# Small products in TensorE's opening pauses, and a weight difference moved behind the turned context's lower halves

## The chip, the cores and the metric

One core of a Trainium2 chip runs the whole program. The metric is the device time in microseconds of one execution, the median of three. TensorE (PE) does the matrix products, ScalarE (ACT) and VectorE (DVE) the element work, GpSimd (POOL) small things, and SyncE (SP) issues nearly all weight loads.

## The reference, cut to what matters

The model is a first block with an adaptive norm, followed by two more layers. Every product is of 256 tokens with a float32 weight. Only the opening matters here: the conditions' modulation and the first gated layer of the context.

```python
def ada_in(x, mod, j, g):
    return rmsnorm(x, g) * (1 + mod[:, 3 * j + 1, None]) + mod[:, 3 * j, None]
...
    sc = jax.nn.silu(c)
    scc = jax.nn.silu(c_ctx)[None]
    mod = (sc @ w_mod[l] + b_mod[l]).reshape(-1, N_MOD, D_MODEL)
    modc = (scc @ w_mod[l] + b_mod[l]).reshape(1, N_MOD, D_MODEL)
...
    xc = ada_out(xc, swiglu(ada_in(xc, modc, 0, norm_pre[l, 0]), ffn_w_in[l, 0], ffn_w_out[l, 0]),
                 modc, 0, norm_post[l, 0], 0.5)
```

`w_mod` has 1024 rows and 9 x 1024 columns, `ffn_w_in` 1024 rows and 2 x 2816 columns.

## The kernel before, in words

**Precision.** A float32 product is made of three faster ones. A factor is split into an upper half (rounded, `whi` for weights, `cTh` for the context) and a lower half (the difference, `wlo`, `cTl`). ScalarE makes the upper halves, VectorE the lower ones with one subtraction each (`Vector.fill`, L2134, for weights; `lo`, L2202, for activations). TensorE then does upper x upper, lower x upper and upper x lower.

**Loads.** SyncE brings weights into a ring of four raw buffers of 1 MB (`Sync`, L725). In this text the loads are counted from 0. Loads 0 to 3 are pieces of `w_mod`, load 4 is the first piece of `ffn_w_in`, loads 5 to 8 are `w_mod` again, and loads 9, 10, 11 are `ffn_w_in`. Load n goes where load n-4 was, so SyncE waits until that one has been read: for a `w_mod` piece by TensorE, for an `ffn_w_in` piece until VectorE has made the lower halves of both its parts. SyncE waits in order: a late load holds back all behind it. An `ffn_w_in` load is two dma instructions of 512 KB and holds two parts ("parts" 0 and 1 in load 4, 2 and 3 in load 9, 4 and 5 in load 10, 6 and 7 in load 11).

**Modulation.** `Tensor.mod` makes 512 columns of a modulation from two loads. For each it issues four products of the 32 columns of `m.sct` (the conditions, of which two columns are filled) with 512 columns of raw float32 weight, into the four groups of 32 rows of one bank. VectorE adds the bias (`modr`, L2278), and `Tensor.settle` brings the rows into columns (the `selm` products, 128x2). VectorE copies them to `modc` (the shift, L2339) or makes `gcol` of them (the gain, L2342).

**The opening's order.** `Tensor.first_block` runs modulation 0 (loads 0, 1) and 1 (loads 2, 3), turns the normed context with sixteen transposes (L992) into four banks (`sh0`), does modulation 2 (loads 5, 6), then part 0, modulation 3 (load 7, the settling of 2, load 8), part 1, the settling of 3, and parts 2 to 7 back to back (`OPENING`). A part is 24 products of 128x256 and waits (`split`) for its own lower half. Parts 0 to 3 read the context's first four column blocks ("half 0"), parts 4 to 7 the last four ("half 1"). No product is done without data of its own being there, so TensorE stands still between the first loads.

`Vector.first_block` (L2498 and on) runs twice over a half. In each round it adds the biases, makes the weight differences of two parts (`force(2 + 2 * half)`), settles the gain, multiplies and shifts a turned half (L2247) while ScalarE does the other token tile (L1602), and takes the context's lower halves (`cTl`) of both tiles after ScalarE's `cTh`.

Of the kernel before, what the change touches and what calls it, by code (L numbers as in the profile page):

```python
# [90 lines left out]
class Tables:  # L91
# [96 lines left out]
    def mod(self, nb, bank=None):  # L188
        self.take("mod", nb, bank=bank)
        self.mod_units[nb] = len(self.units)  # L190
        for kh in range(2):
            self.mod_read[len(self.units)] = (nb, kh, len(self.mod_units))
            self.unit([(slice(0, 2048), 4, self.I["w_mod"][kh * 512:kh * 512 + 512, nb * 512:nb * 512 + 512].rearrange("(k p) n -> p k n", p=128))], 0, 0)
        self.settle()
        self.open = nb
# [686 lines left out]
class Tensor:  # L882
# [139 lines left out]
        elif s in (0, 2):  # L1022
            self.e.wait_ge(self.m.xt_done, self.ready[i] - (s == 0))

    def mod(self):
        m, e = self.m, self.e
        n, nb = self.nmod, MODS[self.nmod]
        u0 = self.t.mod_units[nb]
        if n == 0:
            e.wait_ge(m.c_silu, 1)  # L1030
        bank, full = self.bank("mod", nb)
        for kh in range(2):
            e.wait_ge(m.raw_in[(u0 + kh) % NRAW], self.t.raw_value[u0 + kh])
            for k in range(4):
                ins = self.mm(bank[32 * k:32 * k + 32, :], m.sct[:, 4 * kh + k, :], m.raw[:, (u0 + kh) % NRAW, k * 512:k * 512 + 512],
                              kh == 0, kh == 1)
            ins.then_inc(full if kh else m.mod_half, 1)
            if kh == 0:
                self.settle()
        self.nmod += 1  # L1040

    def settle(self):
# [86 lines left out]
    def first_block(self):  # L1129
        m, e = self.m, self.e  # L1130
        cT, xT = (m.cTh, m.cTl), (m.xTh, m.xTl)
        self.mod()
        self.mod()
        e.wait_ge(m.ld_ident, 16)
        for half in range(2):
            for i in range(2):
                e.wait_ge(m.normed, 2 * i + half + 1)
                self.turned(("sh0", 2 + i), half, m.zc[:, i, :])
                self.settle()
        self.nn, self.nx = 4, 4  # L1140
        self.mod()
        for n, (g, kh) in enumerate(OPENING):
            e.wait_ge(m.xt_done, 4 if kh else 2)
            for v in range(2):
                self.sub_w(2 * n + v, ("up", "c", g), 2 * kh + v, cT, 256, 4, 2, 512)
                if n == 0:
                    if v == 0:
                        self.mod()
                    else:
                        self.settle()  # L1150

        def ahead_c(g):
            if 4 <= g < EARLY:
                self.mod()
        self.hidden("c", cT, 2, ahead_c, lambda g: None, between={
            4: lambda: self.shape_z(("sh0", 0), 0), 7: lambda: self.shape_z(("sh0", 1), 1), 12: lambda: self.summed(10)})
        self.own(2, 0)
        self.own(2, 1)
        self.hidden("x", xT, 0, lambda g: None, self.beside, 6, {(1, 2 * NG - 6 + 4): lambda: self.shape_z(("sh1", 0), 0)},
                    {12: lambda: self.summed(12)})  # L1160
        self.latent()
        self.renewed(2)
        order = [(("wo1", half), 2 * kh + v, 2 * (1 - kh) + v) for kh in (1, 0) for half in range(2) for v in range(2)]
        self.product([("wo1", 0), ("wo1", 1)], xT, 2, 4, 2, 512, self.mixed, tail=6, order=order, hooks={
            (0, 3): lambda: self.heads("ml", m.Mh, 1), (0, 5): self.settle, (1, 6): lambda: self.shape_z(("sh", 1, 0), 0)})
        self.ffn(1, xT, lambda i: self.shape_z(("sh", 1, i), i), lambda: self.shape_x(("sh", 2, 0), 0), 6, 6, (5, 4))
# [936 lines left out]
class Vector:  # L2103
# [376 lines left out]
    def first_block(self):  # L2480
        m, e = self.m, self.e
        e.memset(m.brow[:, :, :], 0.0).then_inc(m.dve, 1)
        e.memset(m.sct[:, :, :], 0.0).then_inc(m.dve, 1)
        e.memset(m.cols[:, NCOL:NCOL + 2], -0.5).then_inc(m.dve, 1)
        for _ in range(3):
            self.step()
        e.wait_ge(m.ld_cols, 16)
        self.normalize()
        self.mod()
        self.normalize()  # L2490
        for half in range(2):
            if half:
                self.mod()
            self.mod()
            self.force(2 + 2 * half)
            self.settle()
            self.evacuated("mod2", half, 0)
            self.evacuated("mod2", 2 + half, 0)  # L2498
            self.shift(("sh0", 3), half, 0, 1)
            for i in range(2):  # L2500
                self.shifted(m.cTl, m.cTh, i, (half,))
        self.stream(8, between={5: lambda: self.hide("c", 0)})
        self.hide("c", 1)
        for g in range(2, NG):
            if 4 <= g < EARLY:
                self.mod()
            self.stream(4)
            self.settle()
            self.hide("c", g)
            if g in (6, 7):  # L2510
                self.normalize()
        e.memset(m.selm[:, 130:258], 1.0).then_inc(m.dve, 1)
        self.step()
        self.hidden(NG - 1)
        st, floor = [self.stat() for _ in range(2)], [0, 0]

        def weigh(half, i):
            c = slice(half * 512, half * 512 + 512)
            self.squared()
            bank, free = self.held("dn", "c", 0, half, i)  # L2520
            e.tensor_tensor(m.z[:, i, c], bank[:, :], m.gp[:, 1, c], ALU.mult).then_inc(free, 1)
            if half == 0:
                e.tensor_scalar(st[i][:, 0:1], st[i][:, 0:1], D * EPS, None, ALU.add).then_inc(m.dve, 1)
                floor[i] = self.step()

        for u in range(2 * NG):
            self.force(self.used + 1)
            if u == NG - 1:
                for i in range(2):
                    weigh(0, i)  # L2530
            self.use()
            if u in (4, 7):
                self.shape(("sh0", u // 5), 0, 0, (m.xTh, m.xTl))
            if u == 15:
                self.summed(10)

        def post(i):
            weigh(1, i)
            for half in range(2):
                self.evacuated("dn", "c", 0, half, i)  # L2540
            self.post(m.xc[:, i, :], m.z[:, i, :], st[i], 0.5, floor[i])

        beside = {0: {0: lambda: post(0), 2: self.normalize}, 1: {0: lambda: post(1), 2: self.normalize},
                  5: {0: lambda: self.biased("c", m.Rc), 1: lambda: self.conv1(m.uPc, m.uc), 2: lambda: self.logged("c", m.Rc, 1)},
                  6: {0: lambda: self.run("c", m.Rc, 0, m.po_dve), 2: self.context_out},
                  7: {1: lambda: self.context_values(0)}, 8: {1: lambda: self.context_states(0), 2: lambda: self.context_values(1)},
                  9: {1: lambda: self.context_states(1)}}
        for g in range(NG):
            self.stream(4, between=beside.get(g, {}))
            if g == 0:  # L2550
                self.summed(11)
            self.hide("x", g)
            self.beside(g)
        self.hidden(NG - 1)
        gp = [[m.gp[:, n, :]] * 2 for n in range(2)]
        self.last(NG, [[("dn", "x", 0, half, i) for i in range(2)] for half in range(2)], gp[0], True,
                  lambda: self.shape(("sh1", 0), 1, 0, (m.xTh, m.xTl)), 6, "x", between={15: lambda: self.summed(12)})
        self.latent()
        self.last(4, [[("wo1", half, i) for i in range(2)] for half in range(2)], gp[1], True,
                  lambda: self.shape(("sh", 1, 0), 2, 0, (m.xTh, m.xTl)), 6, "wo1", late=True)  # L2560
        self.ffn(1, False, gp[0], False, lambda: self.gained(("sh", 2, 0), 0), 6, 6, 5, "ffn1")
# [503 lines left out]
```

## Time and profile before

| | us |
|---|---|
| median of three runs (lowest, highest) | 2028.65 (2028.09, 2030.54) |
| the profiled execution's own time | 2027.45 |
| its span, first to last instruction | 2025.6 |
| TensorE busy in it | 1993.3 (98%) |

Times of the trace count from the first instruction. The span lacks 1.85 us of what the execution is timed at. The first 50 us hold all that the change touches.

### The profile page before, as it was taken

Reading aid. Unit: us, or ns where it says so; the run is one execution under the profiler, and the core shown is the slowest. Engines: PE = TensorE matmul, PEld = TensorE weight load, DVE = VectorE, ACT = ScalarE, POOL = GpSimd, SP = SyncE. Lnnn points to the kernel's source line nnn. Section 1 sums busy time; section 2 is a strip of 40 time slices with the busy share of each in tenths; the row PEclk is TensorE's granted clock in tenths of the full one; section 3 lists DMA queues with packets and bytes.
Section 4 is the critical chain, followed back from the end, with each engine's and each line's share of the span. In section 5 each row is a group of like instructions: output and inputs, shape, how many; then the busy total and the mean of one; then the engine's idle time right before and its main releaser. Section 6 shows DMA issues by size and latency. Waiting matters only on the chain.

```text
span 2025.6 us, 27588 instructions
## 1 busy us (share of the span) xinstructions
PE 1993.3 (98%) x10892; PEld 1687.4 (83%) x10892; DVE 1351.2 (67%) x2199; ACT 1104.2 (55%) x1722; POOL 60.3 (3%) x125
## 2 busy tenths in 40 slices
PE   7999999999999999999999999999999999999998
PEld 5988899988678888888997888888888897788887
DVE  4457676666787656655598896655665587987653
ACT  4344465445565446554646766545654646666552
POOL 0000000001000000000100000000000100000000
PEclk9999999999999999999999999999999999999999
DMA  9797755675268656655543466555755534457551
GB/s 338 257 299 255 238 188 178 213 256 174 96 203 259 208 176 216 196 177 198 199 143 125 141 217 218 187 178 161 233 177 202 203 117 150 142 189 237 187 179 51
DMA packets 281905, 392.90 MB, mean 194 GB/s; under 512 B 9612, under 2 KB 175932, under 8 KB 281648
## 3 DMA queue, kind: packets, MB, share of 16 engines
q1 hardware_dynamic: 277616, 379.62, 57.0%
q0 software_dynamic: 3184, 9.02, 1.4%
q10 hardware_dynamic: 976, 2.49, 0.3%
q8 instruction: 87, 1.43, 0.3%
q14 instruction: 42, 0.34, 0.0%
HBM read 390.04 MB, written 1.05 MB: 193 GB/s over the span
## 4 chain that ended last, share of the span: by engine, by line
PE 83%; DVE 6%; issue 4%; DMA 3%; ACT 3%; POOL 0%; SPq 0%; DVEq 0%; POOLq 0%; ACTq 0%
PE bank L944 20%; PE bank L946 20%; PE bank L945 20%; PE bank L908 19%; DMA raw<-in_ffn_w_in 2%; DVE wlo L2134 1%; PE bank L1084 1%; DVE junk L2837 1%; PE bank L992 1%; ACT whi L1531 1%; DMA raw<-in_w_mod 1%; DVE wlo L2139 1%; ACT whi L1536 0%; DVE tm L2994 0%; ACT junk L1591 0%
## 5 line engine op out<-in xcount | busy, mean ns | idle before, releaser
L2134 DVE TENSOR_TENSOR wlo<-raw,whi 128x1024 fp32r<-128x1024 f32 x360 | 435.4, 1223 | 279.1 <-ACT whi L1531 273.3
L1531 ACT ACTIVATE whi<-raw 128x1024 fp32r<-128x1024 f32 x360 | 376.5, 1058 | 381.7 <-PE bank L946 223.4
L944 PE MATMUL bank<-whi,xTh 128*128 128x512 f32 (+1 forms) x1344 | 528.7, 393 | 3.9 <-DVE xTl L2202 2.0
L946 PE MATMUL bank<-whi,xTl 128*128 128x512 f32 (+1 forms) x1344 | 520.6, 387 | 0.0
L945 PE MATMUL bank<-wlo,xTh 128*128 128x512 f32 (+1 forms) x1344 | 520.1, 387 | 0.0
L2139 DVE SCALAR_TENSOR_TENSOR wlo<-raw,cols,whi 128x512 fp32r<-128x512 f32 (+2 forms) x608 | 407.1, 722 | 149.7 <-ACT whi L1536 146.4
L1536 ACT ACTIVATE whi<-raw,cols 128x512 fp32r<-128x512 f32 (+2 forms) x608 | 385.6, 696 | 147.0 <-PE bank L946 110.4
L944 PEld LDWEIGHTS bank<-whi,xTh 128*128 128x128 f32 x1344 | 252.6, 188 | 57.4 <-issue 4.4
L946 PEld LDWEIGHTS bank<-whi,xTl 128*128 128x128 f32 x1344 | 252.4, 188 | 52.4
L945 PEld LDWEIGHTS bank<-wlo,xTh 128*128 128x128 f32 x1344 | 252.8, 188 | 48.9 <-issue 0.5
L908 PE MATMUL bank<-xTh,whi 128*128 128x256 f32 x696 | 197.9, 284 | 0.0
L908 PE MATMUL bank<-xTl,whi 128*128 128x256 f32 x696 | 196.9, 283 | 0.0
L908 PE MATMUL bank<-xTh,wlo 128*128 128x256 f32 x696 | 196.9, 283 | 0.0
L944 PE MATMUL bank<-whi,hThb 128*128 128x512 f32 x352 | 138.0, 392 | 0.0
L946 PE MATMUL bank<-whi,hTlb 128*128 128x512 f32 x352 | 137.1, 389 | 0.0
L945 PE MATMUL bank<-wlo,hThb 128*128 128x512 f32 x352 | 137.0, 389 | 0.0
L908 PEld LDWEIGHTS bank<-xTh,whi 128*128 128x128 f32 x696 | 133.5, 192 | 1.2 <-issue 1.0
L908 PEld LDWEIGHTS bank<-xTl,whi 128*128 128x128 f32 x696 | 133.5, 192 | 0.4 <-issue 0.2
L908 PEld LDWEIGHTS bank<-xTh,wlo 128*128 128x128 f32 x696 | 133.5, 192 | 0.0
L908 PE MATMUL bank<-cTh,whi 128*128 128x256 f32 x392 | 112.5, 287 | 1.2 <-DVE wlo L2134 1.1
L908 PE MATMUL bank<-cTl,whi 128*128 128x256 f32 x392 | 110.9, 283 | 0.0
L908 PE MATMUL bank<-cTh,wlo 128*128 128x256 f32 x392 | 110.8, 283 | 0.0
(372 smaller groups left out, 2432.8 us busy)
## 6 DMA issues: line engine op xcount, KB each, us to landing
raw<-in_w_in SPq DMA_DIRECT2D x68, 1024.0 KB, 5.2
raw<-in_ffn_w_in SPq DMA_DIRECT2D x132, 512.0 KB, 5.7
raw<-in_ffn_w_gate SPq DMA_DIRECT2D x88, 512.0 KB, 4.1
raw<-in_ffn_w_up SPq DMA_DIRECT2D x88, 512.0 KB, 5.1
raw<-in_ffn_w_down SPq DMA_DIRECT2D x40, 1024.0 KB, 5.0
raw<-in_w_mod SPq DMA_DIRECT2D x36, 1024.0 KB, 5.3
raw<-in_ffn_w_out SPq DMA_DIRECT2D x30, 1024.0 KB, 5.7
raw<-in_w_out SPq DMA_DIRECT2D x12, 1024.0 KB, 5.1
```

Of the source, the lines that this page charges most:

```text
L908: return self.e.matmul(o, lhsT, rhs, start=start, stop=stop, skip_group_check=True)
L944: e.matmul(o, hi[:, kc, sl], wh[:, c], start=at == 0 and k == 0, stop=False)
L945: e.matmul(o, hi[:, kc, sl], wl[:, c], start=False, stop=False)
L946: ins = e.matmul(o, lo[:, kc, sl], wh[:, c], start=False, stop=fin)
L992: ins = self.e.transpose(bank[:, c * 128:c * 128 + 128], src[:, k * 128:k * 128 + 128], self.m.ident[:, :])
L1084: ins = e.transpose(bank[:, (2 * c + i) * 128:(2 * c + i + 1) * 128], htok[:, 2 * (g % 2) + i, c * 128:c * 128 + 128], m.ident[:, :])
L1531: e.activation(wh, raw, ACT.Copy).then_inc(m.whi_done, 1)
L1536: ins = e.activation(wh[:, c], raw[:, c], ACT.Copy, scale=m.cols[:, a + k:a + k + 1])
L2134: e.tensor_tensor(wl, raw, wh.bitcast(F32), ALU.subtract).then_inc(m.wlo_done, 1)
L2139: ins = e.scalar_tensor_tensor(out=wl[:, c], in0=raw[:, c], scalar=m.cols[:, a + k:a + k + 1], in1=wh[:, c].bitcast(F32), op0=ALU.mult, op ...
L2837: ins = e.scalar_tensor_tensor(out=y[:, c, :], in0=m.uC[:, c, j:j + 256], scalar=w_, in1=y[:, c, :], op0=ALU.mult, op1=ALU.add)
```

## The change

`Tensor.warm` issues a number of products of 32 by 256 columns of `m.sct` with itself, into the four row groups of the bank in which the last turned half will be put later; nothing reads their results. There are 28 of them behind modulation 0's first half, 8 behind its second, and 8 behind modulation 1's first half (and the settling of modulation 0 that follows that).

In `Vector.first_block` each round now makes only the first of its two weight differences ahead of the shift; the second stands behind the context's lower halves. In round 0 that is the difference of part 1, in round 1 that of part 3. ScalarE's order and TensorE's order of everything else stay.

```diff
+    def warm(self, count):
+
+        m = self.m
+        bank = m.psum[self.t.bank["sh0", 3, 1][0]]
+        for k in range(count):
+            self.mm(bank[32 * (k % 4):32 * (k % 4) + 32, 0:256], m.sct[:, k % 8, :], m.sct[:, :, :].rearrange("p k s -> p (k s)"), True, True)
+
-    def mod(self):
+    def mod(self, fill=(0, 0)):
...
             if kh == 0:
                 self.settle()
+            self.warm(fill[kh])
...
-        self.mod()
-        self.mod()
+        self.mod((28, 8))
+        self.mod((8, 0))
         e.wait_ge(m.ld_ident, 16)
...
             if half:
                 self.mod()
             self.mod()
-            self.force(2 + 2 * half)
+            self.force(1 + 2 * half)
             self.settle()
             self.evacuated("mod2", half, 0)
             self.evacuated("mod2", 2 + half, 0)
             self.shift(("sh0", 3), half, 0, 1)
             for i in range(2):
                 self.shifted(m.cTl, m.cTh, i, (half,))
+            self.force(2 + 2 * half)
```

## Rows read from the trace of the kernel before

**Rows 1.** The page: busy time of each engine over the span.

```profile
PE 1993.3 (98%) x10892; PEld 1687.4 (83%) x10892; DVE 1351.2 (67%) x2199; ACT 1104.2 (55%) x1722; POOL 60.3 (3%) x125
```

**Rows 2.** Chain of waits, 0 to 120 us: start, length, engine and line.

```profile
26.34 12.09 PE bank L908 x96
...
44.74 23.28 PE bank L908 x192
```

**Rows 3.** Timeline of TensorE: start, length, instruction, count, idle time before it.

```profile
6.96 1.93 PE L908 MATMUL bank<-raw,sct 128*32 128x512 f32 x8 [6.96 <-DMA raw<-in_w_mod]
12.73 1.94 PE L908 MATMUL bank<-raw,sct 128*32 128x512 f32 x8 [3.84 <-DMA raw<-in_w_mod]
15.33 1.94 PE L908 MATMUL bank<-raw,sct 128*32 128x512 f32 x8 [0.67 <-DMA raw<-in_w_mod]
17.20 1.87 PE L908 MATMUL bank<-selm,modr 128*128 128x2 f32 x8
...
23.54 2.80 PE L992 MATMUL bank<-ident,zc 128*128 128x128 f32 x12
...
28.48 0.39 PE L908 MATMUL bank<-cTh,whi 128*128 128x256 f32 x1
...
31.54 1.06 PE L908 MATMUL bank<-raw,sct 128*32 128x512 f32 x8
...
32.54 1.05 PE L908 MATMUL bank<-selm,modr 128*128 128x2 f32 x8
...
38.43 0.36 PE L908 MATMUL bank<-cTh,whi 128*128 128x256 f32 x1
```

**Rows 4.** Windows of the trace: busy time of each engine, granted clock, DMA share, GB/s.

```profile
13.00:15.00 2.00, 1.67 (x8) 0.00 (x0) 1.42 (x8) 1.75 (x6) 0.00 (x0) 1.00 1.05 387
...
28.00:30.00 2.00, 2.00 (x20) 1.52 (x13) 1.03 (x2) 0.00 (x0) 0.29 (x1) 1.00 1.05 385
...
46.00:48.00 2.00, 2.00 (x19) 2.00 (x18) 2.00 (x2) 0.24 (x2) 0.00 (x0) 1.00 0.58 177
```

**Rows 5.** Timeline of SyncE's issues: loads 6, 7, 8, and one issued at 53 us.

```profile
17.33 0.37 SPq L725 DMA_DIRECT2D raw<-in_w_mod  x1
...
20.99 0.37 SPq L725 DMA_DIRECT2D raw<-in_w_mod  x1
...
24.65 0.37 SPq L725 DMA_DIRECT2D raw<-in_w_mod  x1
...
53.10 0.37 SPq L725 DMA_DIRECT2D raw<-in_w_mod  x1
```

**Rows 6.** The same four issues in the DMA view: size, us to landing.

```profile
raw<-in_w_mod SPq DMA_DIRECT2D x1, 1024.0 KB, 9.5
...
raw<-in_w_mod SPq DMA_DIRECT2D x1, 1024.0 KB, 8.4
...
raw<-in_w_mod SPq DMA_DIRECT2D x1, 1024.0 KB, 7.5
...
raw<-in_w_mod SPq DMA_DIRECT2D x1, 1024.0 KB, 5.2
```

**Rows 7.** Timeline of VectorE and ScalarE, 21 to 46 us.

```profile
22.26 2.36 DVE L2134 TENSOR_TENSOR wlo<-raw,whi 128x1024 fp32r<-128x1024 f32 x2 [0.36 <-ACT whi L1531]
...
27.05 1.29 DVE L2202 TENSOR_TENSOR cTl<-full,cTh 128x512 fp32r<-128x512 f32 x2 [0.82 <-ACT cTh L1585]
...
36.02 2.01 ACT L1531 ACTIVATE whi<-raw 128x1024 fp32r<-128x1024 f32 x2 [8.48 <-DMA raw<-in_ffn_w_in]
...
37.11 2.36 DVE L2134 TENSOR_TENSOR wlo<-raw,whi 128x1024 fp32r<-128x1024 f32 x2 [1.52 <-ACT whi L1531]
...
41.89 1.29 DVE L2202 TENSOR_TENSOR cTl<-full,cTh 128x512 fp32r<-128x512 f32 x2 [0.83 <-ACT cTh L1585]
...
43.37 4.63 DVE L2134 TENSOR_TENSOR wlo<-raw,whi 128x1024 fp32r<-128x1024 f32 x4 [0.18 <-ACT whi L1531]
```

**Rows 8.** Waits of SyncE, 0 to 30 us: total, times, longest.

```profile
SPq L725 <- DVE wlo L2134: 3.3, 1, 3.3
```

## The prediction

> **What bounds the kernel now.** The page comes first: TensorE is busy for 98% of the span [rows 1], so a microsecond won or lost in its queue is won or lost at the end, unless a transfer or another engine takes it back on the way. The chain of waits says where this holds in the opening: from 26.34 to 38.43 us and from 44.74 to 68.02 it runs in TensorE alone [rows 2]. Nothing that moves the start of parts 4 to 7 (44.74) is hidden behind them, and the four raw buffers tie the later loads to TensorE's own progress. So the question is when part 4 starts.
>
> The timeline shows two things ahead of that. TensorE waits for `w_mod` three times: 6.96, 3.84 and 0.67 us [rows 3]. And the same eight records of a modulation half take 1.93 us at first and 1.06 us at 31.54, the settling 1.87 and 1.05 us [rows 3]. Early TensorE works at half its later rate, that of the lower of its two clock levels, although the windows print a granted clock of 1.00 throughout [rows 4]; I go by the durations. Under all this lies a third bound: the DMA engines are fully used, 387 GB/s at 13 us and 385 at 28, and let up only at 46 us (share 0.58) [rows 4]. A load then lands when those ahead of it have landed, whenever TensorE becomes ready.
>
> **Step 1, the small products.** A modulation half is four products of 512 columns in 1.93 us; four of 256 columns should take half, about 0.97 at the low rate and 0.53 at the high one. 28 are seven such groups: 3.7 us if all are fast, 6.8 if all are slow. The pause is 3.84 us. Work at the low rate ran from 12.73 to 26.3 without the rate rising, but it held a gap of 0.67 us and settlings that stream two columns [rows 3]. The small products make an unbroken stretch of real streaming from 6.96 us on, so I take it that the rate doubles somewhere in them, that they end near 13 to 14.5 us, and that TensorE is fast from there. Cost at this point: up to 2 us on load 1's products, and load 5 is issued later by as much; load 4 and those ahead keep the DMA busy meanwhile, so this is hidden. The two groups of eight cost 2 x 0.53 us each and lie in waits for loads 2 and 3. Bounds: nothing, or (all slow) the rival below.
>
> What does the faster rate bring? Modulation 2's second load, 6, is issued at 17.33 and lands 9.5 us later, at 26.83 [rows 5, 6]. Its products then take 1.06 us, to 27.9, where part 0 starts today at 28.48 [rows 3]. The gain is at most 0.6 us, because the DMA sets the rest. This is the term in which the whole first edit ends.
>
> **Step 2, round 0 of VectorE.** The two differences start at 22.26 and take 2.36 us [rows 7]. With one of them moved, the shift and the context's lower halves come 1.2 us earlier: they end at 27.05 + 1.29 = 28.34 now, and at about 27.15 then. That is before 27.9, so it allows the 0.6 us of step 1 and no more. Part 1's difference then ends at about 28.35; TensorE wants part 1 only after part 0 and modulation 3, beyond 34 us, so for TensorE it is hidden.
>
> It isn't for SyncE. Load 8 goes where load 4 was and waits for both differences: that is SyncE's wait of 3.3 us on `wlo` [rows 8], ended at 24.65 [rows 5]. Now it ends at 28.4. Load 7, the one ahead, lands at 20.99 + 8.4 = 29.4 [rows 5, 6], so the queue holds one microsecond of work, a fresh load shows 5.2 us from issue to landing [rows 6], and load 8 lands at 28.4 + 5.2 = 33.6 instead of 24.65 + 7.5 = 32.15: 1.45 us late. Loads 9, 10 and 11 are issued behind it. The bound below is no gap at all (28.4 is still before 29.4), that above 1.45 us for load 9 too. I take 1.0, nearer to the fresh load's row. The Trainium skill, "DMA: Bandwidth & Descriptors", section on the anatomy of one DMA, fits a fixed 2.0 us and then bytes at 436 GB/s; by its 4.4 us for this load, load 8 would be only 0.7 us late and my total below 0.3 to 0.5 us smaller. The trace's 5.2 us is of a HBM-to-SBUF load of exactly this size and disagrees, so I keep it.
>
> On TensorE: part 0 27.9 to 30.8 (2.9 us, as (38.43 to 44.3) / 2), load 7's products and the settling 1.06 + 1.05 to 32.9, then 0.7 us of waiting for load 8, its products to 34.7, part 1 to 37.6, the settling to 38.6. Part 2 started at 38.43. The 0.6 us are gone.
>
> **Step 3, round 1 of VectorE.** Here the moved difference is that of part 3, and part 3 follows part 2 directly. Today VectorE takes both from 37.11 to 39.47 [rows 7], part 2 runs 38.43 to 41.3, part 3 finds its difference there. Then comes the context: from the end of the differences (39.47) to the end of `cTl` (41.89 + 1.29 = 43.18) pass 3.7 us. After the change the first difference ends at 38.3, plus load 9's lateness of 1.0 is 39.3; the context's lower halves end at 43.0; part 3's difference, 1.2 us more, at 44.2; part 3 starts at 44.35 (the step from 44.59 to 44.74 today [rows 2, 7]) and not at 41.3. TensorE stands still for 2 us. Part 4 starts 2.9 later, at 47.25, against 44.74: **+2.5 us**. What the edit brings forward, the lower halves of half 1 for part 4, isn't late today by more than the third of a microsecond before 44.74, and part 4's own difference still queues behind part 3's. With no gap in the DMA the same sum gives 38.3 + 3.7 + 1.2 + 0.15 + 2.9 = 46.25, +1.5; with 1.45 us it gives +3.0.
>
> **Sum.** 0 for steps 1 and 2, +2.5 for step 3 with the late load in it: 2027.45 + 2.5 = 2029.95. The profiled execution was 1.2 us quicker than the median. I add 0.35 of that, because I expect part of the 1.2 to be a rate that rises later than in this profile, which the small products would end, and say 2030.3, 0.08% above the median.
>
> **Rivals.** *Faster: the late rise was the common case.* In the profile the rate is still low at 23.5 us, where twelve transposes take 2.80, and the next modulation half at 31.54 is fast [rows 3]. The three runs spread over 2.45 us. If in most executions the rate rises only during parts 0 and 1, the kernel before loses up to 2.9 us there (a part at half rate takes 2.9 more), and the change gives it back. With 2 us of it, and no DMA gap (+1.5), the end is 2028.65 - 2 + 1.5 = 2028.1. It decides from 1.5 us on. For it: the median above the profiled time; against: only by 1.2. Chance 0.14.
>
> *The rate falls again.* Faster products leave longer pauses, about 2 us between modulation 2's halves. If part 0 and modulation 3 then run at the low rate, that is 2.9 + 1.1 + 1.0 more, of which 0.7 lie in the wait for load 8 and the rest delays part 2 by up to 4; the rise comes back on the way, so I count half, 2 us in part 2, 1 of them under load 9's lateness: 2031.3. The Trainium skill's "TensorE: Matmul & The Clock Gate", part on the PE-mode transpose, says that transposes do not count as activity, which would favour this rival, as they lie right before. The trace here speaks against it: the stretch before the rate rose was made mostly of them. Chance 0.11.
>
> *The small products don't do what they are for.* They run slow and don't raise the rate: 6.8 us in a pause of 3.84, and 1.9 for each eight. Load 1's products start at 15.7, modulation 1 ends near 26, the transposes near 31.7, part 0 starts 5 us later than today, and part 4 some 6 later: 2034. Chance 0.07.
>
> **Chances.** My forecast has 0.68 with a range of its own of 2028.9 to 2031.8 (+1.5 to +3.0 on the profiled time, and up to 1.2 for how it stands to the median). A difference of about 0.2% (4.1 us) is what a measurement of this kernel can tell from none. Only the last rival passes it on the slow side: with tails 0.09 slower. Faster by 4.1 us isn't reached even by the first rival: 0.03. The rest, 0.88, is within. The range of 2027.7 to 2032.8 reaches into the first two rivals and leaves out the third.
>
> **What would show it.** Right: seven groups of small products whose length halves on the way; load 6's products in 1.06 us and part 0 at 27.9; SyncE's issue of load 8 near 28.4 and its landing near 33.6; a wait of TensorE of about 2 to 3 us on `wlo` near 42 us; part 4 near 47. Wrong: TensorE without a wait before part 3, load 8 landing at 32.2 as before, small products that keep 0.97 us per group, or parts 0 and 1 at half rate.

## The result: 2033.08 us, 0.24% slower

The changed kernel takes 2033.08 us in the median of seven runs (2030.23 to 2035.97), the kernel before 2028.65 in seven. The ratio is 1.0024 with a 95% interval of 1.0015 to 1.0033. The forecast was 2030.3 with a range to 2032.8: right in direction, too small in size. Measured once more beside other kernels (`after_again`) the ratio was 1.0018 (1.0009 to 1.0027).

The profiled execution took 2034.81 us, 7.36 more than that of before, span 2033.0 against 2025.6. Most of it, 6.1 us, is made in the opening. First TensorE's timeline in the changed kernel (columns as in [rows 3]).

```profile
8.57 3.94 PE L908 MATMUL bank<-sct 128*32 128x256 f32 x56
12.61 1.07 PE L908 MATMUL bank<-raw,sct 128*32 128x512 f32 x8
...
15.21 1.06 PE L908 MATMUL bank<-raw,sct 128*32 128x512 f32 x8 [0.68 <-DMA raw<-in_w_mod]
...
25.09 1.07 PE L908 MATMUL bank<-raw,sct 128*32 128x512 f32 x8 [2.66 <-DMA raw<-in_w_mod]
27.67 1.94 PE L908 MATMUL bank<-raw,sct 128*32 128x512 f32 x8 [1.52 <-DMA raw<-in_w_mod]
29.54 0.58 PE L908 MATMUL bank<-cTh,whi 128*128 128x256 f32 x1
...
34.53 1.07 PE L908 MATMUL bank<-raw,sct 128*32 128x512 f32 x8
...
46.47 0.39 PE L908 MATMUL bank<-cTh,whi 128*128 128x256 f32 x1 [2.06 <-DVE wlo L2142]
```

The small products do what they are for: the modulation half that took 1.94 us at 12.73 takes 1.07, and the groups fit their pauses. But new pauses of 2.66 and 1.52 us stand beside modulation 2, and its second half runs at 1.94 us again. The windows of the same kernel (columns as in [rows 4]) show the clock behind this.

```profile
24.00:27.00 3.00, 1.07 (x8) 0.19 (x8) 2.08 (x8) 2.43 (x7) 0.00 (x0) 1.00 1.05 384
28.00:30.00 2.00, 2.00 (x10) 0.46 (x3) 1.61 (x3) 0.00 (x0) 0.00 (x0) 0.50 0.20 72
30.00:32.00 2.00, 2.00 (x11) 2.00 (x11) 0.47 (x1) 0.00 (x0) 0.52 (x1) 0.50 0.74 160
34.00:36.00 2.00, 2.00 (x18) 1.03 (x17) 0.00 (x0) 0.00 (x0) 0.00 (x0) 1.00 1.10 369
44.00:47.00 3.00, 0.94 (x8) 0.74 (x7) 3.00 (x4) 3.00 (x4) 0.00 (x0) 1.00 0.67 211
48.00:50.00 2.00, 2.00 (x11) 2.00 (x11) 1.82 (x2) 0.00 (x0) 0.00 (x0) 0.50 0.98 304
52.00:54.00 2.00, 2.00 (x19) 2.00 (x18) 1.23 (x1) 0.19 (x1) 0.00 (x0) 1.00 0.99 324
```

The granted clock is 0.50 (1.2 GHz) in the rows from 28 to 32 us and once more at 48, behind a stretch in which TensorE stood still (0.94 of 3 us busy). While it is low, TensorE does 10 or 11 products in 2 us instead of 18 to 20. The share of the DMA is 0.20 at 28 to 30 us where it was 1.05 [rows 4]: the gap ahead of load 8. VectorE and ScalarE answer to [rows 7].

```profile
22.21 2.00 ACT L1539 ACTIVATE whi<-raw 128x1024 fp32r<-128x1024 f32 x2 [3.11 <-DMA raw<-in_ffn_w_in]
...
26.95 1.29 DVE L2210 TENSOR_TENSOR cTl<-full,cTh 128x512 fp32r<-128x512 f32 x2 [0.82 <-ACT cTh L1593]
28.16 1.22 DVE L2142 TENSOR_TENSOR wlo<-raw,whi 128x1024 fp32r<-128x1024 f32 x1
...
38.73 1.23 DVE L2142 TENSOR_TENSOR wlo<-raw,whi 128x1024 fp32r<-128x1024 f32 x1 [0.16 <-ACT whi L1539]
...
43.99 1.29 DVE L2210 TENSOR_TENSOR cTl<-full,cTh 128x512 fp32r<-128x512 f32 x2 [0.82 <-ACT cTh L1593]
45.20 4.62 DVE L2142 TENSOR_TENSOR wlo<-raw,whi 128x1024 fp32r<-128x1024 f32 x4
```

Load 4's upper halves begin at 22.21; the kernel before, in `before_again`, has them at 21.28 and every kernel without small products at 21.1 to 21.3. So load 4 lands 1 us later, which the forecast did not have. The last row is part 3's difference and those behind it: it starts where the lower halves end, and TensorE waits 2.06 us for it. SyncE's wait for load 4's differences is 9.8 us, not 3.3 [rows 8]:

```profile
SPq L725 <- DVE wlo L2142: 9.8, 1, 9.8
```

The ledger, in starts on TensorE after minus before: part 0 +1.06 (29.54 against 28.48), of which 0.9 is modulation 2's half at the low clock; modulation 3's first half, behind part 0, +2.99 (34.53 against 31.54), so part 0 costs 1.93 more; then 2.06 us of waiting for part 3, 1.7 for 3.4 us at the low clock behind it, and less 0.33, the wait ahead of part 4 that goes. That sums to 6.4; the settling of the fourth modulation group, at 92.91 us before, comes at 99.04, +6.13, so the terms overlap by 0.3 us. This ledger is of one execution, one of the slower ones; the median of the runs is only 4.4 us above that of before. A later settling, at 254.22, comes at 261.58: +7.36, the whole difference.

### The profile page after: what moved, and what is told of

The parts are those of the page before. It is cut to its first block, busy times and chain, and to the rows that moved or that the text cites. A ratio compares the mean times of both kernels' runs of the same rounds, so it can differ in the third digit from the quotient of the medians.

```text
span 2033.0 us, 27764 instructions
## 1 busy us (share of the span) xinstructions
PE 1997.1 (98%) x10980; PEld 1690.9 (83%) x10980; DVE 1351.6 (66%) x2199; ACT 1104.6 (54%) x1722; POOL 60.0 (3%) x125
## 3 DMA queue, kind: packets, MB, share of 16 engines
HBM read 390.04 MB, written 1.05 MB: 192 GB/s over the span
## 4 chain that ended last, share of the span: by engine, by line
PE 83%; DVE 6%; issue 4%; DMA 3%; ACT 3%; SPq 0%; POOL 0%; DVEq 0%; POOLq 0%; ACTq 0%
PE bank L944 20%; PE bank L946 20%; PE bank L945 20%; PE bank L908 20%; DMA raw<-in_ffn_w_in 2%; DVE wlo L2142 1%; DMA raw<-in_w_mod 1%; PE bank L1092 1%; DVE junk L2846 1%; ACT whi L1539 1%; PE bank L992 1%; DVE wlo L2147 1%; SPq L725 0%; ACT whi L1544 0%; DVE tm L3003 0%
```

## The experiments

Two settlings of TensorE's timeline serve as marks: one near 93 us, just behind the parts of the opening and before the loads of the next stage get scarce, and one near 254 us. The marks and the waits between are from one profile each, the ratios from all runs. Two executions of the kernel before differ by 0.2 us at the first mark and 1.1 at the second.

| kernel | mark at 93 | mark at 254 | ratio to before (95% interval) |
|---|---|---|---|
| before / `before_again` | 92.91 / 93.12 | 254.22 / 253.14 | 1.0005 (0.9995, 1.0015) |
| changed / `after_again` | 99.04 / 95.98 | 261.58 / 258.25 | 1.0024 (1.0015, 1.0033) / 1.0018 (1.0009, 1.0027) |
| `e1_fill` | 93.89 | 255.22 | 1.0009 (1.0000, 1.0018) |
| `e2_move` | 96.13 | 256.55 | 1.0014 (1.0005, 1.0023) |
| `e4_move1` | 96.06 | 256.36 | 1.0014 (1.0005, 1.0023) |
| `e7_hold` | 93.17 | 256.63 | 1.0017 (1.0008, 1.0026) |
| `e8_hold_move` | 96.06 | 258.18 | 1.0032 (1.0023, 1.0041) |
| `e9_hold_late5` | 93.34 | 255.84 | 1.0017 (1.0008, 1.0026) |
| `e10_mid` | 93.23 | 253.29 | 1.0003 (0.9995, 1.0012) |
| `e13_fat` | 94.04 | 256.64 | 1.0010 (1.0001, 1.0019) |
| `e15_tiny` | 93.27 | 254.91 | 1.0007 (0.9998, 1.0015) |
| `e14_fat_mid` | 92.58 | 255.32 | 1.0008 (0.9999, 1.0017) |

The first theory was that two things cost: the clock falling in the pauses that fast products leave, and part 3 standing still for its difference.

**One half each.** `e1_fill` keeps the small products and puts VectorE's order back, `e2_move` does the reverse, `e4_move1` moves only part 3's difference, without small products.

```diff
 e1_fill:             self.force(2 + 2 * half)
 e2_move, e4_move1:   self.mod((0, 0))
                      self.mod((0, 0))
 e4_move1:            self.force((1 if half == 1 else 2) + 2 * half)
                      ...
                      self.force(2 + 2 * half)
```

> Only the small products; VectorE's order as in the kernel before. Theory A (TensorE's rate falls in the pauses that faster products leave): the granted clock rises within the 28 small products, falls to 0.50 near 27 us after two pauses beside modulation 2, part 0 runs at the low rate; part 3 finds its difference and no second fall follows; part 4 near 47 to 48 us instead of 44.74, about +2 to +3 us in the end. Rival B (only the moved difference costs): part 4 at 44.7 or earlier, time within 0.5 us of before. Rival C (earlier issue of load 5 makes load 4 and 6 land later): load 4's upper halves start near 22.2 us instead of 21.2 and modulation 2's second half near 27.7 here too.

> Only the moved differences, in both rounds; no small products. Theory A: the early clock is as in the kernel before (it rises somewhere from 27 to 31 us), part 3 waits about 2 us for its difference and the clock may fall once after this wait; part 4 near 46.5 without a second fall and near 48 with one: +1.8 to +3.5 us. Rival B: the whole loss of the change is here, +4.4 us or more. Rival C: load 4's upper halves start at 21.2 as before.

> Only round 1's difference (part 3) moved; no small products. Theory A: all of the loss of e2_move is in this round, because round 0's move costs only a late load 8 that TensorE does not feel: same time as e2_move within 1 us. Rival D (load 8 held back in round 0 costs as much): this kernel is 1 us or more faster than e2_move, with load 9 landing at 36 here and at 37 there.

`e1_fill` runs modulation 2's second half low again (27.71, 1.93 us), does not wait for part 3, and is 1.0 us late at the first mark, less than the 2 to 3 us expected. Its load 4 is late too (upper halves at 22.41), which is the sign of rival C. `e2_move` waits 1.71 us for part 3 and is 3.2 late there; `e4_move1` waits as long and is 3.15 late. Two of TensorE's rows with an idle time in `e2_move`, and `e4_move1`'s wait for part 3 with the clock behind it:

```profile
34.82 1.06 PE L908 MATMUL bank<-raw,sct 128*32 128x512 f32 x8 [0.90 <-DMA raw<-in_w_mod]
...
45.04 0.39 PE L908 MATMUL bank<-cTh,whi 128*128 128x256 f32 x1 [1.71 <-DVE wlo L2142]
```

```profile
43.49 0.39 PE L908 MATMUL bank<-cTh,whi 128*128 128x256 f32 x1 [1.76 <-DVE wlo L2142]
```

```profile
44.00:47.00 3.00, 3.00 (x16) 3.00 (x16) 2.83 (x3) 0.33 (x1) 0.00 (x0) 0.51 0.73 228
```

The two sums have different terms: `e2_move` pays 0.90 us for the late load 8 and starts part 3 at 45.04, without a fall of the clock; `e4_move1` starts it at 43.49, and the clock falls behind the wait (0.51 in its row of that window). The times came as expected (2031.28 and 2031.41 us), the reasons only in part: TensorE does feel the late load 8, and part 4 starts at 48.02 us in `e2_move` though its clock did not fall. That the two times agree is partly luck, since one has a fall and the other a late load. By the marks the moved differences cost more (3.2 us) than the small products (1.0 us); the ratios, 1.0014 and 1.0009, point the same way, but their intervals overlap. Of the 3.15 us of `e4_move1`, 1.7 are its fall, by the count of the ledger above.

**The change again, and the clock held.** `after_again` is the changed kernel unchanged. `e7_hold` adds small products to `e1_fill` beside modulation 2, `e8_hold_move` adds them to the whole change.

```diff
         self.nn, self.nx = 4, 4
+        self.warm(20, ("mod", MODS[1]))
-        self.mod()
+        self.mod((12, 0))
```

> The changed kernel once more, for a second profile. Theory A: the clock falls near 27 us again, for 3.4 or 6.8 us, and part 3 waits about 2 us; the parts ahead of 80 us come 4 to 6 us later than before. Rival E (the low rate from 27 us was chance and is not in most executions): clock at 1.00 from about 10 us to 44 us, and the total 2 to 3 us above before.

> The small products of the change, 20 more ahead of modulation 2 and 12 between its halves, into the bank that modulation 1 used; VectorE's order as before. Theory A: the clock stays at 1.00 from the first rise on, modulation 2's second half takes 1.06 us, part 0 starts near 28.5, part 4 at 44.7: time within 1 us of before, 0 to 2 us faster than e1_fill less 2 to 3. Rival B: no difference from e1_fill. If small products cost TensorE more than the pauses hold, part 0 starts later than 28.7.

> The whole change, with 20 more small products ahead of modulation 2 and 12 between its halves. Theory A (standstill of part 3 plus low rate after pauses): the clock does not fall near 27 us; part 3 still waits 2 us or more for its difference and the clock may fall once after that; the second modulation load of the fourth group is read near 82 to 83.5 us, against 85.6 in the changed kernel and 79.45 before; time 2 us below the changed kernel. Rival B (the moved difference alone costs all): as the changed kernel.

In `after_again` the clock does not fall in the opening. Its rows are nearly those that the forecast had worked out:

```profile
27.78 1.06 PE L908 MATMUL bank<-raw,sct 128*32 128x512 f32 x8 [1.55 <-DMA raw<-in_w_mod]
28.77 0.39 PE L908 MATMUL bank<-cTh,whi 128*128 128x256 f32 x1
...
34.68 1.06 PE L908 MATMUL bank<-raw,sct 128*32 128x512 f32 x8 [0.80 <-DMA raw<-in_w_mod]
...
44.90 0.38 PE L908 MATMUL bank<-cTh,whi 128*128 128x256 f32 x1 [1.70 <-DVE wlo L2142]
```

So rival E holds in part: the fall near 27 us is in some executions and not in others of the same program. The two falls make the 3.1 us between the two profiles at the first mark; without them the change still loses 3.1 us there.

How much the falls matter to the medians can be read from the mean granted clock that is on record for every run (what lies ahead of the first change counts as 1.00 in it). A single fall of 3.4 us makes it 0.999, so a run at 1.000 had none. Two runs of `after_again` have 1.000 and took 2031.7 us; the six runs of before beside them that have 1.000 have a median of 2027.3. So without any fall the change costs 4.4 us, no less than by the medians. Falls do come more often with the change: 8 of its 17 runs have 0.998 or less, and 16 of 99 runs of the kernel before. In the same way `e2_move` costs 2.9 us without a fall and `e7_hold` 3.5, `e14_fat_mid` 0.9 and `e10_mid` (the last two stand below) 0.3, from two to four runs each. Of the 4.4 us the moved differences are thus 2.9, and the small products 1.5 on top, by these few runs.

`e7_hold` keeps the clock and missed all the same: it was to be within 1 us of before, is on time at the first mark (+0.3), and ends at 1.0017. It starts part 0 at 29.39 us, because load 4 is late, and it loses 2.1 us more than before between the marks, in waits for weight differences in the stage of scarce loads (the waits of TensorE from 60 to 160 us, `e7_hold` first, then the kernel before):

```profile
PE bank L908 <- DVE wlo L2143: 2.8, 3, 1.5
```

```profile
PE bank L908 <- DVE wlo L2134: 0.8, 1, 0.8
```

`e8_hold_move` missed: 0.1 us from `after_again` at the marks, and no faster than the changed kernel. Its ratio is the highest of all, though its interval overlaps that of the changed kernel. Holding the clock is not worth its products.

**Why load 4 lands late.** The first guess was load 5: TensorE reads load 1 sooner, so load 5 is issued 1 us earlier and shares the DMA with load 4. `e9_hold_late5` is `e7_hold` with SyncE waiting for modulation 1's first half before it issues load 5.

```diff
+            if u == 5:
+                e.wait_ge(m.mod_half, 2)
```

> As e7_hold, but SyncE also waits for the end of modulation 1's first half (some 16.3 us) before it issues load 5. Theory C (load 5, issued 1 us earlier because its buffer is read earlier, shares the DMA engines with load 4 and delays it): load 4's upper halves start at 21.2 instead of 22.2, the context's lower halves of half 0 end near 28.3, part 0 starts at 28.4 instead of 29.4; 1 us faster than e7_hold. Rival (load 4 is late for another reason, such as the small products' own traffic): load 4 still at 22.2.

Refuted: load 5 is issued at 16.55 us, later than the 14.73 of the kernel before, and load 4's upper halves still start at 22.30. The queue table then showed what all kernels with the 44 small products or more share, and none without them: a block of instructions fetched between 15 and 21 us (changed kernel, 18 to 21; packets, MB, share of sixteen engines).

```profile
q8 instruction: 1, 0.02, 2.4%
```

2.4% of sixteen engines over 3 us is 1.15 us of one engine. If a load has landed only when the last of its engines has, an engine of a busy sixteen that loses 1.15 us delays it by as much. That one engine is behind shows where the others run dry, in the gap ahead of load 8 (windows of the changed kernel, then of `e2_move`, which has no early fetch):

```profile
28.50:30.00 1.50, 1.50 (x10) 0.46 (x3) 1.11 (x2) 0.00 (x0) 0.00 (x0) 0.50 0.06 22
```

```profile
28.70:29.10 0.40, 0.40 (x6) 0.29 (x3) 0.04 (x1) 0.00 (x0) 0.00 (x0) 1.00 0.02 5
```

A DMA share of 0.06 is one engine of sixteen, and 22 GB/s is about a sixteenth of the 385 before. It goes on for 1.5 us, and load 7 lands at 30.3 (issued at 19.18, 11.1 us); in `e2_move` it lands at 29.35 (20.95 and 8.4). `e2_move`'s own block is fetched between 28.7 and 30.1 us, while its load 8 is on the way, and that load takes 6.1 us where those of the changed kernel and `after_again` take 5.2 and 5.1.

In the kernel before the first such block comes after 30 us. Two kernels, both with VectorE's order as before, test what brings it forward: `e13_fat` has 20 products of 512 columns in place of 44 of 256, `e15_tiny` 44 of 2 columns.

```diff
 e13_fat:   self.mod((12, 4))
            self.mod((4, 0))
            rhs: m.sct[:, 0:1, :].to_broadcast([128, 16, 32])
 e15_tiny:  rhs: m.sct[:, 0, 0:2]
```

> As e1_fill, but the small products are 20 of 512 columns (12, 4, 4) instead of 44 of 256: about the same time on TensorE with 80 instead of 176 more records. Theory F (the longer program makes TensorE's next block of instructions be fetched at 16 to 20 us, in the middle of saturated loads, and one DMA engine of the sixteen then ends load 4 late): the fetch moves behind 24 us, load 4's upper halves start at 21.2 instead of 22.3, the context's lower halves of half 0 end at 28.3. Rival G (the small products' own reading of the memory slows the DMA): load 4 still at 22.3, since they stream as much.

> As e1_fill, but each of the 44 small products streams 2 columns: the same 176 more records and nearly no streaming. Theory F: a fetch of instructions at 16 to 20 us and load 4's upper halves at 22.3, with the early clock as before (low until 27 us or later); part 0 1 us later than before, about 1 us slower in the end. Rival G: load 4 at 21.2, time as before.

ScalarE's first upper halves in `e13_fat` and then in `e15_tiny`:

```profile
21.17 2.00 ACT L1539 ACTIVATE whi<-raw 128x1024 fp32r<-128x1024 f32 x2 [2.04 <-DMA raw<-in_ffn_w_in]
```

```profile
22.29 2.00 ACT L1539 ACTIVATE whi<-raw 128x1024 fp32r<-128x1024 f32 x2 [3.05 <-DMA raw<-in_ffn_w_in]
```

Both came as expected. The fetch is at 30 to 33 us in the first and at 18 to 21 in the second. In `e13_fat` load 6 is there by 26.66 us too, where the changed kernel waits for it until 27.67. Nearly as many streamed columns (10240 for 11264) do no harm, as many instructions with hardly any columns do. The number of TensorE's instructions, not their work, makes load 4 late, by 1.1 us. `e13_fat` is no faster than `e1_fill` for all that: in its profile the clock was at the low level from 25.7 us, modulation 2's second half took 1.93 us, and part 0 ran low.

**Another place for the difference.** `e10_mid` has no small products and puts the second difference between VectorE's shift and its lower halves; `e14_fat_mid` adds the 20 wide products.

```diff
             self.shift(("sh0", 3), half, 0, 1)
+            self.force(2 + 2 * half)
             for i in range(2):
                 self.shifted(m.cTl, m.cTh, i, (half,))
```

> No small products; the second difference stands between VectorE's shift and its lower halves, in both rounds, where VectorE waits 0.8 us for ScalarE anyway. Theory A: part 3's difference ends near 41.1 and part 3 starts without a wait near 41.3, the lower halves of half 1 end 0.8 us earlier than before, and the wait of 0.33 us ahead of part 4 goes: part 4 at 44.3, time 0 to 1 us below before. Load 8 is issued near 26.3. Rival (any difference behind the shift costs): 1 us or more slower than before.

> The 20 products of 512 columns and the second difference between the shift and the lower halves, as in e10_mid. Theory F: load 4 at 21.2, part 3 without a wait, no wait ahead of part 4; the same as before or up to 1.5 us faster where the clock holds, 1 to 2 us slower in executions where it falls near 27 us.

VectorE in `e10_mid`, round 1:

```profile
40.71 1.21 DVE L2142 TENSOR_TENSOR wlo<-raw,whi 128x1024 fp32r<-128x1024 f32 x1
41.84 1.28 DVE L2210 TENSOR_TENSOR cTl<-full,cTh 128x512 fp32r<-128x512 f32 x2
43.08 4.63 DVE L2142 TENSOR_TENSOR wlo<-raw,whi 128x1024 fp32r<-128x1024 f32 x4
```

The difference fills VectorE's 0.8 us of waiting, neither part 3 nor part 4 waits, and VectorE's chain is 0.3 us ahead of [rows 7] although it began 0.85 later (37.96 against 37.11, as load 9 came later). TensorE pays for that load: part 2 starts at 39.29, not 38.43, and part 4 at 45.12, not at the 44.3 expected. At 1.0003 the interval holds 1: no gain or loss that the runs can tell. `e14_fat_mid` is the only kernel ahead of before at the first mark (0.3 us; part 0 starts at 27.64 us, which is what the forecast had hoped for), and it gives that back in 2.1 us of waits at 96, 134 and 150 us: 1.0008, so it missed too. No version beat the kernel before.

## Why the forecast was wrong in size

In short: the step that failed is step 1, where the small products were priced at nothing outside their pauses. In runs without any fall of the clock the whole change costs 4.4 us and the moved differences alone 2.9, against the 2.5 of the forecast; the small products are the missing term, 1.5 us, and the marks show where: `after_again` and `e2_move` are equal at the first (95.98 and 96.13), and 1.7 us apart at the second (258.25 and 256.55). What lies between is waiting for weight differences, 1.6 us in the one and none in the other.

- *What bounds the kernel*: right. What the opening lost stayed lost: +6.13 at 93 us and +7.36 in the end. A lead is kept less well: part 0 started 0.88 us sooner in before than in `before_again`, and of that 0.2 us were left at the first mark.
- *Step 1, small products as such*: right. 3.94 us, the rate doubling within them, a modulation half in 1.07 us.
- *Step 1, no cost elsewhere*: wrong. The forecast priced streaming and left out that 44 products are 176 more records in TensorE's program. Their fetch makes load 4 1.1 us late and load 6 land near 27.7 us instead of 26.83, so part 0 starts at 28.77 at best, not at 27.9. By itself that costs little, 0.3 to 0.4 us at the first mark (`e7_hold`, `e15_tiny`). The larger cost is the waiting behind the opening, which every kernel with added products has.
- *Step 2*: right for the first time of load 8: issued at 28.66 in `e2_move`, 28.4 forecast, and at 29.52 in `after_again`, the difference being load 4's. A fresh load took 5.1 us there against 5.2 in [rows 6]. The 4.4 us estimated by the fit in the Trainium skill ("DMA: Bandwidth & Descriptors", anatomy of one DMA) is shorter than both; that section is on DMAs that GpSimd issues, and SyncE issues these. TensorE's wait for it was 0.80 us, 0.7 forecast.
- *Step 3*: right in mechanism, and nearly in size. Part 3 starts at 44.90 in `after_again` (44.35 forecast) after 1.70 us of waiting, and part 4 at 47.87 (47.25 forecast).
- *The rival of the falling rate*: mis-sized too, but not what puts the median off. It had a chance of 0.11 and 1 us. In the profiled execution the clock fell twice, the second time behind part 3's wait, which the forecast did not consider; together about 4.5 us on TensorE (0.9 + 1.93 + 1.7), of which 3.1 are left at the first mark. A fall stood behind that wait in `e4_move1` too, without small products, and none in `e2_move`, `e8_hold_move` and `after_again`, so the wait alone does not decide it. The Trainium skill ("TensorE: Matmul & The Clock Gate", PE-mode transpose) leads one to expect the low rate behind transposes; the windows show a fall in the profile and none in `after_again`, which prints 1.00 from 24 to 54 us, behind the same transposes.
- *The rival of the late rise*: small. `before_again` has both halves of modulation 2 in 3.00 us against 2.28, and is 0.2 us later at the mark.
- *What stays open*: in kernels with added products TensorE waits 1.2 to 2.8 us for differences between 90 and 156 us (the waits of one profile each, summed), in those without 0 to 0.8. More instructions shift later fetches too, but no experiment isolates this. And what decides, from execution to execution, whether the clock falls was not found.

## What to carry to other kernels

A difference, copy or cast that is moved behind another step must be followed to its own reader: here part 3 follows 2.9 us behind part 2, and its difference ends 5.4 us later (39.47 to 44.84), 4.0 of them by the move alone (43.43 in `e4_move1`), the rest by late loads. Where an engine waits for another inside its own chain (0.8 us here), that is the place for it. Filler instructions are not free even in a pause: they are program, and here the program's blocks were fetched through the DMA engines that the loads had full. And a faster stretch ahead of a bound that does not move only makes pauses; in some executions the clock fell again in them. Last, a profile is one execution: the account has to fit the runs without its accidents too.

## What the runs showed of the hardware

- One fetched block of instructions (0.02 MB, 1.15 us of one DMA engine) in a saturated stretch makes a 1 MB load of sixteen engines land 1.1 us late (`e15_tiny` against `e13_fat`), and one engine of sixteen is still at work when the others are done.
- The granted clock of the view starts at 1.00 until its first change: before 27 us in [rows 4] it prints 1.00 while the durations are those of half the rate (1.93 us for a modulation half, 1.06 later).
- The length of the pauses beside modulation 2 does not by itself decide the fall of the clock: it fell with pauses of 2.66 and 1.52 us (changed kernel) and with 1.45 and 1.70 (`e13_fat`), and stayed with 1.42 and 1.55 (`after_again`) and with 1.33 and 1.71 (`e14_fat_mid`). It also fell for 3.4 us near 540 us in seven of the fourteen profiles, `before_again` among them, which is noise of 1.7 us between them:

```profile
535.00:545.00 10.00, 9.37 (x52) 8.48 (x51) 4.46 (x19) 2.48 (x3) 0.00 (x0) 0.83 0.00 0
```

That row is of `e2_move`; in the first profile of before the same window prints 1.00.
